# The two projections of 16 columns multiplied in split form, with high and low weights side by side in 32 columns

## The chip, the cores and the metric

The kernel runs on one core of one Trainium2 chip. The metric is the time of one execution on the device, in microseconds (us); lower is better. Engines are called as the profile calls them: PE is TensorE's matmul (PEld its weight load), DVE is VectorE, ACT is ScalarE, POOL is GpSimd, SP is SyncE, which here only issues DMAs.

## What is computed

Two transformer blocks on 256 rows of 1024 features. The first has, beside its wide projections, one of 16 columns, the low-rank factor of a gate; the second has, beside its wide ones, 16 columns of logits (8 `b_logit`, 8 `a_logit`) for the gated delta rule. Cut to what matters:

```
h = rms_norm(x, norm_w)
proj = h @ w_in                          # (256, 1024) @ (1024, 6160)
(gq, gk, gv, glr, hq, hf, hi, xq, gate) = split(proj)      # glr has 16 columns
glr_up = glr @ gla_w_gate_up + gla_b_gate                  # (256, 16) @ (16, 512)
gla_log_a = log_sigmoid(glr_up) / 16

h2 = rmsnorm(h, n[2])                    # 272 rows: 16 meta tokens and 256
proj = h2 @ w_in_2
u_f, u_sc, u_qkv, z, b_logit, a_logit, gate_logit = split(proj)   # 8 + 8 columns
beta = sigmoid(b_logit);  g = -exp(A_log) * softplus(a_logit + dt_bias)
```

## The kernel before

Activations lie transposed in SBUF: features on the 128 partitions in `KT` = 8 tiles, rows of the sequence along the free axis (256, or 272 with the meta tokens). Weights come in panels of 128 output columns by 1024 features (512 KB), through a ring of four slots: SP loads `raw`, ACT rounds it to float32r (`whi`, L722), POOL takes the rest (`wlo` = `raw` - `whi`, L622, two instructions of 128x512 for one panel). Activations are split in the same way into `xh` and `xl`. A wide output is then three float32r products for each of the eight tiles (`whi`x`xh`, `whi`x`xl`, `wlo`x`xh`), 24 matmuls summed in one PSUM bank `panel` (`products`, L1659). Four banks `panel` and four banks `aux` are used in rotation. Where a slot or a bank comes free, and where one is full, is told by semaphores (`lo_ready`, `passed`, `bank_free`, `aux_free`, `aux_full`).

The order of steps is written out by hand in `first_schedule` and `mixer_schedule`; each engine walks the same list and does its own part of each step. The two narrow projections stand apart from the panels:

- `("lowrank",)` is the first step of the first list. PE multiplies plain float32: 8 matmuls with `wglr` (16 columns) as weights and `tmp`, the normed input, moving (L1783). The profile records each float32 matmul as two. DVE copies the result to `glr` (L1185). The step `("decay",)`, after the first 16 outputs, multiplies `glr` by `upw` (L1793).
- `("ba",)` stands in the second list behind `("qkv", 0)`, a step that computes three outputs abreast. PE multiplies `wba` by `h` in float32 (L1953), with 272 rows moving; DVE had scaled `wba` by the gains much earlier (L1178). DVE multiplies the result by `xrstd` into `ba` (L1378). `("logits",)` transposes `ba` four times on PE (L1960), `DVE` and `ACT` turn the logits into `grate` (last at L1389, semaphore `g_ready`), and `("cumulate",)` sums `grate` on PE (L1967, L1968).

Ahead of the first list DVE has a series of small instructions on `small1` (L1169 to L1173), then folds a gain vector (L1176) and scales `wba` (L1178). In the list its part of the outputs 0 to 3 is two instructions each on `f` and `k` (L1192, L1193). POOL splits the first panels of this stage (panels 4 to 7, outputs 0 to 3), then clears `s` (a MEMSET, L648), and goes on with panel 8. PE's own part of the first list begins behind these waits:

```
            pe.wait_ge(more_in, 11 * 16)
            pe.wait_ge(split_low, 8)
            for step in FIRST:
```

## Time and profile before

| | us |
|---|---|
| median of 3 runs (lowest, highest) | 1028.63 (1028.36, 1029.28) |
| the profiled execution, its own time | 1030.11 |
| its span, from the first to the last instruction | 1028.3 |
| PE busy | 1004.7 |
| POOL busy | 765.5 |
| DVE busy | 534.0 |
| ACT busy | 486.5 |

The profile is of one execution. Its span is 1.8 us shorter than that execution's own time, and that time is 1.5 us above the median of the three runs. Times in the rows below are counted from the start of the span. The engines work beside each other, so their busy times don't add up; the chain of waits tells which of them set the end at each moment.

### The profile page before, as it was taken

Reading aid. Unit: us, or ns where it says so; the run is one execution under the profiler, and the core shown is the slowest. Engines: PE = TensorE matmul, PEld = TensorE weight load, DVE = VectorE, ACT = ScalarE, POOL = GpSimd, SP = SyncE. Lnnn points to the kernel's source line nnn. Section 1 sums busy time; section 2 is a strip of 40 time slices with the busy share of each in tenths; the row PEclk is TensorE's granted clock in tenths of the full one; section 3 lists DMA queues with packets and bytes.
Section 4 is the critical chain, followed back from the end, with each engine's and each line's share of the span. In section 5 each row is a group of like instructions: output and inputs, shape, how many; then the busy total and the mean of one; then the engine's idle time right before and its main releaser. Section 6 shows DMA issues by size and latency. Waiting matters only on the chain.

```text
span 1028.3 us, 21621 instructions
## 1 busy us (share of the span) xinstructions
PE 1004.7 (98%) x8212; PEld 984.2 (96%) x8212; DVE 534.0 (52%) x898; ACT 486.5 (47%) x748; POOL 765.5 (74%) x602
## 2 busy tenths in 40 slices
PE   9999999999999999999999899999999989999996
PEld 7999999999999999999899899999999989999996
DVE  5925984457544444504755463466656464444203
ACT  6543324456654444444566534433255554444441
POOL 2896666657999888996586845577539929999993
PEclk9999999999999999999999899999999999999998
DMA  9563334343565555555462213433226726665561
GB/s 319 163 203 127 123 105 143 119 128 107 181 198 183 175 171 174 165 174 181 126 186 91 72 54 114 142 125 122 85 65 199 215 95 195 195 196 184 173 185 58
DMA packets 48330, 154.62 MB, mean 150 GB/s; under 512 B 6060, under 2 KB 11188, under 8 KB 48264
## 3 DMA queue, kind: packets, MB, share of 16 engines
q1 hardware_dynamic: 46112, 151.31, 47.3%
q10 hardware_dynamic: 2152, 2.38, 0.7%
q8 instruction: 48, 0.79, 0.3%
q14 instruction: 18, 0.15, 0.0%
HBM read 151.57 MB, written 2.10 MB: 149 GB/s over the span
## 4 chain that ended last, share of the span: by engine, by line
PE 88%; DVE 4%; ACT 3%; POOL 2%; issue 1%; DMA 1%; SPq 0%; DVEq 0%; ACTq 0%
PE panel L1659 69%; PE panel L1709 3%; PE aux L1812 2%; POOL wlo L622 2%; PE panel L1759 1%; DMA memk<-in_mem_panels 1%; PE aux L2058 1%; PE aux L2069 1%; PE panel L1745 1%; PE aux L2032 1%; DVE tmp L1080 1%; PE aux L2098 1%; PE aux L2107 1%; PE aux L2021 1%; PE aux L1929 1%
## 5 line engine op out<-in xcount | busy, mean ns | idle before, releaser
L622 POOL TENSOR_TENSOR wlo<-raw,whi 128x512 fp32r<-128x512 f32 x554 | 736.4, 1358 | 239.7 <-ACT whi L722 221.3
L1659 PE MATMUL panel<-xh,whi 128*128 128x256 f32 (+1 forms) x1440 | 417.9, 290 | 4.7 <-DVE xl L1069 4.1
L1659 PE MATMUL panel<-xh,wlo 128*128 128x256 f32 (+1 forms) x1440 | 411.1, 285 | 0.0
L1659 PE MATMUL panel<-xl,whi 128*128 128x256 f32 (+1 forms) x1440 | 410.4, 285 | 0.0
L722 ACT ACTIVATE whi<-raw 128x1024 fp32r<-128x1024 f32 x280 | 293.9, 1053 | 217.7 <-PE panel L1659 184.3
L1659 PEld LDWEIGHTS panel<-xh,whi 128*128 128x128 f32 x1440 | 273.7, 190 | 7.3 <-issue 4.2
L1659 PEld LDWEIGHTS panel<-xh,wlo 128*128 128x128 f32 x1440 | 273.5, 190 | 0.0
L1659 PEld LDWEIGHTS panel<-xl,whi 128*128 128x128 f32 x1440 | 272.9, 190 | 0.2
L1659 PE MATMUL panel<-hh,wlo 128*128 128x272 f32 (+1 forms) x352 | 100.4, 285 | 0.0
L1659 PE MATMUL panel<-hh,whi 128*128 128x272 f32 (+1 forms) x352 | 100.1, 284 | 0.0
L1659 PE MATMUL panel<-hl,whi 128*128 128x272 f32 (+1 forms) x352 | 99.9, 284 | 0.0
L1339 DVE TENSOR_TENSOR hid<-hid,sil 128x272 f32<-128x272 f32 (+1 forms) x44 | 50.4, 1146 | 44.1 <-ACT sil L898 44.1
L1120 DVE TENSOR_SCALAR tmp<-panel,vec 128x256 f32<-128x256 f32 (+1 forms) x24 | 11.7, 489 | 107.8 <-ACT sq L779 107.8
L1659 PEld LDWEIGHTS panel<-hh,whi 128*128 128x128 f32 x352 | 66.3, 188 | 0.0
L1659 PEld LDWEIGHTS panel<-hl,whi 128*128 128x128 f32 x352 | 66.3, 188 | 0.0
L1659 PEld LDWEIGHTS panel<-hh,wlo 128*128 128x128 f32 x352 | 66.2, 188 | 0.0
L1335 DVE TENSOR_TENSOR hid<-panel,xrstd 128x272 f32<-128x272 f32 (+1 forms) x44 | 19.0, 432 | 55.9 <-PE panel L1659 55.9
L1341 DVE TENSOR_TENSOR hl<-hid,hh 128x272 f32 (+1 forms) x44 | 30.4, 691 | 32.9 <-ACT hh L900 32.9
L900 ACT ACTIVATE hh<-hid 128x272 f32 (+1 forms) x44 | 18.7, 425 | 57.7 <-DVE hid L1339 57.7
L1659 PE MATMUL panel<-mixh,whi 128*128 128x256 f32 x128 | 36.4, 284 | 0.0
L1659 PE MATMUL panel<-mixl,whi 128*128 128x256 f32 x128 | 35.8, 280 | 0.0
L1659 PE MATMUL panel<-mixh,wlo 128*128 128x256 f32 x128 | 35.8, 280 | 0.0
(328 smaller groups left out, 1580.4 us busy)
## 6 DMA issues: line engine op xcount, KB each, us to landing
raw<-in_panels SPq DMA_DIRECT2D x232, 512.0 KB, 3.6
raw<-in_down SPq DMA_DIRECT2D x32, 448.0 KB, 3.2
raw<-in_down SPq DMA_DIRECT2D x16, 512.0 KB, 3.4
memk<-in_mem_panels SPq DMA_DIRECT2D x4, 512.0 KB, 7.9
memx<-in_mem SPq DMA_DIRECT2D x4, 256.0 KB, 5.7
h<-in_x SPq DMA_DIRECT2D x1, 1024.0 KB, 8.7
spill<-h ACTq DMA_DIRECT2D x1, 1024.0 KB, 4.6
h<-spill ACTq DMA_DIRECT2D x1, 1024.0 KB, 7.2
```

The costliest lines, as they stand in the source:

```text
L622: ins = nc.gpsimd.tensor_tensor(wlo[:, slot, half], raw[:, slot, half], whi[:, slot, half].bitcast(f32), ALU.subtract)
L722: A(whi[:, slot, :], raw[:, slot, :], ACT.Copy).then_inc(hi_ready, 1)
L900: A(hh[:, bass.ds(tile, 1), 0:w].rearrange("p a s -> p (a s)"), hid[:, pair, 0:w], ACT.Copy).then_inc(hid_high, 1)
L1080: TT(tmp[:, t, 0:w], tmp[:, t, 0:w], bc(rstd[:, 0:w], 1, len(tiles[m])), ALU.mult).then_inc(weighed, 1)
L1120: TS(tmp[:, i, 0:w], pb[o % 4][:, 0:w], vcol("gains", at0 + i), factor, ALU.mult, ALU.mult)\
L1335: TT(hid[:, pair, 0:w], pb[2 * pair + 1][:, 0:w], xrstd[:, 0:w], ALU.mult)\
L1339: TT(hid[:, pair, 0:w], hid[:, pair, 0:w], sil[:, pair, 0:w], ALU.mult).then_inc(hid_ready, 1)
L1341: TT(hl[:, bass.ds(tile, 1), 0:w].rearrange("p a s -> p (a s)"), hid[:, pair, 0:w], hh[:, bass.ds(tile, 1), 0:w].rearrange("p a s -> p (a ...
L1659: ins = M(bank[:, 0:w], wt[:, slot, P * t:P * t + P], x[:, kk, c0:c0 + w], start=first and m == 0 and n == 0, stop=last and m == len(pairs ...
L1709: ins = M(pb[(o + rt) % 4][:, 0:2 * P], x[:, kk, P * rt:P * rt + P], wt[:, r:r + 2, P * kk:P * kk + P], start=kk == 0 and n == 0, stop=kk ...
L1745: ins = M(pb[o % 4][:, 0:ROWS], mem_panel(i)[:, P * kk:P * kk + P], memg[:, kk, :], start=kk == 0, stop=kk == KT - 1)
L1812: ins = M(bank[:, P * m:P * m + P], k[:, hd, blk], q[:, hd, blk], start=True, stop=True)
```

## The change

Both narrow projections are done with float32r products. DVE writes a new tile `slim` of 8 x 32 columns: the rounded weights in columns 0 to 15, the rest in columns 16 to 31 (`split_slim`: a rounding copy, a wait for it, a subtraction). PE multiplies `slim` by `xh` and by `xl`, 16 matmuls with 32 weight columns, into 32 partitions of the bank (`slim_products`). The high and the low half are added where the result is used next: `upw` is loaded twice, one copy under the other, so that the product with the 32 rows of `glr` is the sum; and the four transposes of `ba` become four float32 matmuls with a constant of 32 x 16 (`both_parts`, new columns of `sel`). `ba` is now made from `xh` and `xl`, which hold the gains already, so `wba` is not scaled. `slim` is one tile for both: it is filled from `wglr` ahead of the first list and from `wba` once the first product has been read.

The step `("lowrank",)` moves behind the outputs 0 and 1.

```
-    steps = [("lowrank",)]
-    steps += [("out", i) for i in range(16)]
+    steps = [("out", 0), ("out", 1), ("lowrank",)]
+    steps += [("out", i) for i in range(2, 16)]
...
-            TT(wba[:], wba[:], bc(vec[:, VEC_AT["gains"] + 16:VEC_AT["gains"] + 24], 2, 16), ALU.mult).then_inc(wba_scaled, 1)
+
+            def split_slim(n, w_):
+
+                CP(slim[:, :, 0:16], w_[:]).then_inc(slim_high, 1)
+                dve.wait_ge(slim_high, n)
+                TT(slim[:, :, 16:32], w_[:], slim[:, :, 0:16].bitcast(f32), ALU.subtract).then_inc(slim_low, 1)
+
+            split_slim(1, wglr)
...
-                    CP(glr[:], bank[0:16, 0:ROWS]).then_inc(aux_free[n % 4], 1)
+                    CP(glr[:], bank[0:32, 0:ROWS]).then_inc(aux_free[n % 4], 1)
+                    split_slim(2, wba)
...
-                    TT(ba[:], bank[0:16, 0:LEN], xrstd[0:16, :], ALU.mult).then_inc(aux_free[n % 4], 1)
+                    TT(ba[:], bank[0:32, 0:LEN], xrstd[0:32, :], ALU.mult).then_inc(aux_free[n % 4], 1)
...
+            def slim_products(bank, n, w):
+
+                pe.wait_ge(slim_low, n)
+                for kk in range(KT):
+                    for m, x in enumerate((xh, xl)):
+                        ins = M(bank[0:32, 0:w], slim[:, kk, :], x[:, kk, 0:w], start=kk + m == 0, stop=kk == KT - 1 and m == 1)
+                return ins
...
-                    for kk in range(KT):
-                        ins = M(bank[0:16, 0:ROWS], wglr[:, kk, :], tmp[:, kk, 0:ROWS], start=kk == 0, stop=kk == KT - 1)
-                    ins.then_inc(aux_full, 1)
+                    slim_products(bank, 1, ROWS).then_inc(aux_full, 1)
...
-                    pe.wait_ge(wba_scaled, 1)
-                    for kk in range(KT):
-                        ins = M(bank[0:16, 0:LEN], wba[:, kk, :], h[:, kk, :], start=kk == 0, stop=kk == KT - 1)
-                    ins.then_inc(aux_full, 1)
+                    slim_products(bank, 2, LEN).then_inc(aux_full, 1)
...
-                        ins = nc.tensor.transpose(bank[0:CH, 16 * c:16 * c + 16], ba[:, CH * c:CH * c + CH], ident[0:16, 0:16])
+                        ins = M(bank[0:CH, 16 * c:16 * c + 16], ba[:, CH * c:CH * c + CH], both_parts, start=True, stop=True)
```

DVE's list around the first narrow projection, before (`small_99` is `small1`, `aux` the bank of the narrow product):

```order
L1172 TENSOR_SCALAR small_99<-small_99 128x4 [waits dve_order]
L1173 TENSOR_SCALAR small_99<-small_99 128x4
L1176 TENSOR_TENSOR vec<-vec 128x8 [waits more_in,dve_order]
L1178 TENSOR_TENSOR wba<-wba,vec 128x128
L1185 COPY glr<-aux 16x256 [waits aux_full]
L1192 TENSOR_SCALAR f<-f,small_99 128x256 [waits bank_free0]
```

and now:

```order
L1179 TENSOR_TENSOR vec<-vec 128x8 [waits more_in,dve_order]
L1184 CAST slim<-wglr 128x8x16
L1186 TENSOR_TENSOR slim<-wglr,slim 128x8x16 [waits slim_high]
L1203 TENSOR_SCALAR f<-f,small_100 128x256 [waits bank_free0]
L1204 TENSOR_SCALAR k<-k,small_100 128x256
L1203 TENSOR_SCALAR f<-f,small_100 128x256 [waits bank_free1]
L1204 TENSOR_SCALAR k<-k,small_100 128x256
L1195 COPY glr<-aux 32x256 [waits aux_full]
L1184 CAST slim<-wba 128x8x16
L1186 TENSOR_TENSOR slim<-wba,slim 128x8x16 [waits slim_high]
L1203 TENSOR_SCALAR f<-f,small_100 128x256 [waits bank_free2]
```

The scaling of `wba` has gone; two instructions on `slim` stand behind the folded gain, the second with a wait, and two more behind the copy to `glr`, which now comes after the `f` and `k` of outputs 0 and 1.

PE's list where the first narrow projection begins, before (`whi,memgh` and the like belong to the memory projection in front of the list):

```order
L1759 MATMUL panel<-whi,memgl 128x256
L1759 MATMUL panel<-wlo,memgh 128x256
L1783 MATMUL aux<-tmp,wglr 16x256 [waits split_low,more_in]
L1783 MATMUL aux<-tmp,wglr 16x256 x7
L1659 MATMUL panel<-xh,whi 128x256 [waits bank_free0,lo_ready]
```

and now, where the 48 matmuls of outputs 0 and 1 end:

```order
L1670 MATMUL panel<-xh,whi 128x256
L1670 MATMUL panel<-xl,whi 128x256
L1670 MATMUL panel<-xh,wlo 128x256
L1679 MATMUL aux<-xh,slim 32x256 [waits slim_low]
L1679 MATMUL aux<-xl,slim 32x256
```

Fifteen more like the last two follow the first of them, in turn. The narrow product has moved behind two panels and waits for `slim_low`, a semaphore of DVE; the outputs in front of it wait for `lo_ready`, a semaphore of POOL.

## Rows read from the trace of the kernel before

**Rows 1.** The page: busy time of PE, and the shares of the chain by engine.
```profile
PE 1004.7 (98%) x8212; PEld 984.2 (96%) x8212; DVE 534.0 (52%) x898; ACT 486.5 (47%) x748; POOL 765.5 (74%) x602
PE 88%; DVE 4%; ACT 3%; POOL 2%; issue 1%; DMA 1%; SPq 0%; DVEq 0%; ACTq 0%
```
**Rows 2.** Chain of waits: start us, us, what; around both projections.
```profile
35.35 3.56 PE aux L1783 x16
38.91 45.63 PE panel L1659 x384
...
286.68 193.32 PE panel L1659 x1536
...
496.50 3.77 PE aux L1953 x16
500.27 3.21 PE panel L1659 x24
503.48 0.24 PE aux L1960 x4
503.72 6.24 PE panel L1659 x48
...
509.96 0.20 PE aux L1967 x4
```
**Rows 3.** Timeline of POOL, 34 to 45 us: start us, us, what.
```profile
34.71 1.28 POOL L622 TENSOR_TENSOR wlo<-raw,whi 128x512 fp32r<-128x512 f32 x1
...
37.17 1.27 POOL L622 TENSOR_TENSOR wlo<-raw,whi 128x512 fp32r<-128x512 f32 x1
...
42.12 1.43 POOL L622 TENSOR_TENSOR wlo<-raw,whi 128x512 fp32r<-128x512 f32 x1
43.48 1.81 POOL L648 MEMSET s<- 128x2048 f32 x1
```
**Rows 4.** Timeline of DVE, 38 to 55 us.
```profile
38.49 1.20 DVE L1171 TENSOR_TENSOR small<-small 128x4 f32<-128x4 f32 x1
39.72 1.21 DVE L1172 TENSOR_SCALAR small<-small 128x4 f32<-128x4 f32 x1
40.85 0.16 DVE L1173 TENSOR_SCALAR small<-small 128x4 f32<-128x4 f32 x1
41.04 1.14 DVE L1176 TENSOR_TENSOR vec<-vec 128x8 f32<-128x8 f32 x1
42.10 0.28 DVE L1178 TENSOR_TENSOR wba<-wba,vec 128x128 f32<-128x128 f32 x1
...
42.82 2.62 DVE L1192 TENSOR_SCALAR f<-f,small 128x256 f32<-128x256 f32 x1
45.37 1.38 DVE L1193 TENSOR_SCALAR k<-k,small 128x256 f32<-128x256 f32 x1
...
54.48 0.41 DVE L1199 COPY k<-panel 128x256 f32<-128x256 f32 x1
```
**Rows 5.** Stretches: us, busy PE, PEld, DVE, ACT, POOL, granted clock, DMA share, GB/s.
```profile
578.90:582.40 3.50, 1.47 (x14) 1.31 (x12) 1.04 (x3) 2.77 (x7) 3.50 (x6) 0.98 0.52 150
582.40:595.90 13.50, 13.50 (x59) 12.80 (x59) 2.69 (x13) 1.24 (x2) 5.25 (x9) 0.50 0.13 40
824.50:828.00 3.50, 1.30 (x9) 1.13 (x9) 3.50 (x9) 1.84 (x5) 0.00 (x0) 1.00 0.81 269
828.00:831.40 3.40, 3.20 (x16) 3.20 (x16) 3.40 (x8) 3.32 (x10) 0.00 (x0) 0.50 0.03 11
```
**Rows 6.** Timeline of DVE (and one row of POOL), 498 to 510 us.
```profile
499.14 0.50 DVE L1408 SCALAR_TENSOR_TENSOR qkv<-panel,vec,qkv 128x271 f32<-128x271 f32 x1
500.31 0.43 DVE L1378 TENSOR_TENSOR ba<-aux,xrstd 16x272 f32<-16x272 f32 x1 [0.66 <-PE aux L1953]
...
509.10 0.19 DVE L1389 SCALAR_TENSOR_TENSOR small<-small 68x32 f32<-68x32 f32 x1
...
498.60 10.02 POOL L622 TENSOR_TENSOR wlo<-raw,whi 128x512 fp32r<-128x512 f32 x8 [17.48 <-ACT whi L722]
```

More of the change, by code:

```diff
@@ L286, in build @@
         eye17 = at("eye17", take(SUB * SUB), [P, SUB, SUB])
-        sel = at("sel", take(57), [P, 57])
+        sel = at("sel", take(73), [P, 73])
         late = take(2048)
         masks = at("masks", late, [P, 8, P], i32)
-        upw = at("upw", late + 1024, [16, 512])
+        upw = at("upw", late + 1024, [32, 512])
+        slim = at("slim", late + 1664, [P, KT, 32], f32r)
         wglr = at("wglr", late + 1536, [P, KT, 16])
@@ L320, in build @@
         prob = at("prob", ar + 23552, [P, 2, 2, ROWS])
-        glr = at("glr", ar + 24576, [16, ROWS])
+        glr = at("glr", ar + 24576, [32, ROWS])
         small1 = at("small1", ar + 24832, [P, 64])
@@ L355, in build @@
         gt = at("gt", rstd_at, [P, 2, ROWS])
-        ba = at("ba", lnt_at, [16, LEN])
+        ba = at("ba", lnt_at, [32, LEN])
         yh = at("yh", tmp_at, [P, 4, ROWS], f32r)
@@ L383, in build @@
         row_in_block, block_of_row = sel[0:CH, 0:SUB], sel[0:CH, SUB:SUB + 4]
+        both_parts = sel[0:32, 57:73]
         matrix_of, block_of = sel[:, SUB + 4:SUB + 36], sel[:, SUB + 36:SUB + 40]
@@ L421, in build @@
         scaled = sem("scaled")
-        wba_scaled = sem("wba_scaled")
+        slim_high = sem("slim_high")
+        slim_low = sem("slim_low")
         down_squared = sem("down_squared")
@@ L2179, in constants @@
     m = np.arange(P)
-    sel = np.zeros((P, 57), f)
+    sel = np.zeros((P, 73), f)
     sel[:CH, :SUB] = np.arange(CH)[:, None] % SUB == np.arange(SUB)
@@ L2183, in constants @@
     sel[:, SUB + 4:SUB + 36] = m[:, None] % 32 == np.arange(32)
-    sel[:, SUB + 36:] = m[:, None] // 32 == np.arange(4)
+    sel[:, SUB + 36:57] = m[:, None] // 32 == np.arange(4)
+    sel[:, 57:] = m[:, None] % 16 == np.arange(16)
     eye = np.broadcast_to(np.eye(SUB, dtype=f), (P, SUB, SUB))
@@ L2253 @@
     arrays = {"panels": panels, "mem_panels": mem_panels[:4], "down": down, "x": rows(x["x"]), "mem": rows(x["mem"]), "meta": rows(x["meta_tokens_2"]),
-              "vec": np.concatenate([table[n] for n in VEC_AT], 1), "upw": x["gla_w_gate_up"],
+              "vec": np.concatenate([table[n] for n in VEC_AT], 1), "upw": np.concatenate([x["gla_w_gate_up"]] * 2),
               "wglr": glr.reshape(KT, P, 16).transpose(1, 0, 2), "wba": ba.reshape(KT, P, 16).transpose(1, 0, 2),
```

## The prediction

> **What bounds the kernel now.** I read the page first. PE is busy 98% of the span, and PE alone is 88% of the chain that ended last [rows 1]: a microsecond taken from PE's queue is a microsecond off the time, unless what PE does next is not ready. Then I read the chain of waits around the two projections [rows 2]. Both lie on it: sixteen recorded matmuls of 3.56 us at 35.35, sixteen of 3.77 us at 496.50, each between matmuls of panels without a gap. Third come the timelines of POOL and DVE beside the first [rows 3, 4], since the change puts DVE's work in front of PE's there; fourth the same for the second [rows 6]; last the stretches where TensorE's granted clock fell [rows 5], since the change can make PE idle.
>
> All sums below are against the profiled execution: span 1028.3 us, its own time 1030.11 us, which is 1.5 us above the median. They give a difference, which I add to the median, 1028.63 us. A measurement of this kernel can tell about 0.2%, 2.06 us, from no change.
>
> **The matmuls themselves.** A float32r matmul with 256 rows moving takes 45.63 / 384 = 0.119 us, one with 272 rows 193.32 / 1536 = 0.126 us [rows 2]. All of these have 128 weight columns; 32 columns are in no row. Bounds: 0.107 us for 256 rows, if only columns at 2.4 GHz counted (the clock granted there is full speed), and 0.2225 us (3.56 / 16, what each recorded half of a float32 matmul takes) if narrow float32r ran no faster than float32. I take 0.119 and 0.126, since number format and rows moving are those of the panels. Lowrank: 16 x 0.119 = 1.90 against 3.56 us. `ba`: 16 x 0.126 = 2.01 against 3.77. Saved on PE: 1.66 + 1.76 = 3.4 us at most. The logits give some back: four transposes took 0.24; four float32 matmuls are recorded as eight, and four records of such a kind (L1967) take 0.20 [rows 2], so 0.40, or 0.2 more.
>
> **The first place: lowrank moved.** Before, PE did lowrank from 35.35 to 38.91 with what was long ready, then outputs 0 and 1 to 38.91 + 48 x 0.119 = 44.6. Now it is different at three points.
>
> - Output 0 comes first and needs `wlo` of panel 4. POOL's second instruction for it is the one at 34.71, done at 35.99 [rows 3]. PE starts at about 36.1 instead of 35.35: idle 0.75. Output 1 needs panel 5, done at 37.17 + 1.27 = 38.4; PE asks at 38.95, so no wait. Outputs 0 and 1 end at 36.1 + 5.7 = 41.8.
> - Lowrank then needs `slim_low`. DVE's folding of the gain ends at 41.04 + 1.14 = 42.2, later than 41.8 already, and the two instructions on `slim` come behind it [rows 4]. Why DVE is late is in the rows: instructions on 4 elements take 1.2 us each. They end at 39.69, 40.93, 42.18, one POOL instruction (about 1.24 us) apart; each that begins after a wait is held to the next boundary between POOL's instructions, and one that follows without a wait goes straight through (L1173 0.16, L1178 0.28).
> - So the rounding copy, which follows without a wait, ends at about 42.3. The subtraction has a wait in front, so POOL's instruction of 42.12 to 43.55 gets in first. Bounds for the end of the subtraction: 42.65 (42.35 + 0.28 as L1178, if nothing holds it); 45.45 if it is held through POOL's MEMSET as well, as L1192 was, which began to wait at 42.82 and ended at 45.44, behind the MEMSET of 43.48 to 45.29 [rows 3, 4]. Between them is 43.7: the boundary at 43.5 and 0.2 us for its 128 elements. I take 43.7, because it is what L1171 and L1176, instructions of the same kind with two inputs in SBUF, did, while L1192 is a TENSOR_SCALAR.
>
> By that, PE idles from 41.8 to 43.8 and ends lowrank at 45.7 instead of having all this done at 44.6: **+1.1 us**. By the other bounds it is +0.05 and +2.85.
>
> The Trainium skill, page "SBUF — State Buffer", section "Who interferes with whom", says that a DVE instruction with two SBUF inputs contends with a GpSimd instruction that reads SBUF, not with one that only writes. No row here has such an instruction beside a MEMSET, so the trace doesn't show it; by the rule the sum is +1.1, and by the row of L1192 alone it would be +2.85.
>
> What is behind these waits: on PE the whole list, so the 1.1 us moves everything after it. On DVE, the `f` and `k` of outputs 0 and 1 start where they did (45.4), and the copy, the rounding and the subtraction behind them add at most 0.4 + 2 x 1.3 = 3.0 us. The first copy out of a bank (L1199) goes from 54.5 to about 57.5 [rows 4]; the output that needs this bank is output 8, at 45.7 + 6 x 2.85 = 62.8. Covered by 5 us; without that cover it would cost what it is late. Panels 6 and 7 are split before the MEMSET, by 43.55, ahead of need. The removed scaling of `wba` (0.28 us of DVE) and the doubled `upw` (32 KB more by DMA, first used behind output 15) cost and give nothing on PE's path; `glr` of 32 instead of 16 partitions changes no count of elements per partition or of columns moved.
>
> **The second place: ba.** `slim` was filled 440 us earlier: no wait. PE ends `ba` at 496.5 + 2.0 = 498.5 instead of 500.27, output `qkv 3` at 501.6, logits at 502.1, two outputs (6.24 us for 48) at 508.3. Their panels are split in time: POOL does eight instructions in 10.02 us from 498.60, so panels are ready at 501.1 and 503.6 [rows 6]. Then `cumulate` needs `g_ready`. DVE's chain towards it began with `ba` at 500.31, after 0.66 us of idle time; now it follows the last instruction of `qkv 0`, which ends at 499.64, so it begins 0.7 us earlier, and all of DVE and ACT behind it up to L1389 is in series: 509.29 becomes 508.6 [rows 6]. PE starts `cumulate` at about 508.8 (the 0.2 us is what the semaphore and a cold start of PE take) instead of 509.96: **-1.15 us**. PE's own work would have given 1.76 - 0.2 = 1.55. Ends: -0.7 (DVE's shift alone) and -1.6.
>
> **Sum:** +1.1 - 1.15 = -0.05 us: 1028.6. From the bounds without the clock: 0.05 - 1.6 = -1.55 to 2.85 - 0.7 = +2.15.
>
> **The clock** is not in this sum. Behind a stretch with 2.0 us of PE idle (3.50 - 1.47) the granted clock fell to 0.50 for 13.5 us; behind one with 2.2 us idle (3.50 - 1.30) for 3.4 us, in dense panels [rows 5]. That is 1.2 GHz instead of 2.4. The new idle time is 2.0 us, with 0.75 more six microseconds before. One stretch of 3.4 us at half clock in dense panels costs 1.7 us.
>
> **The rivals.**
> - *The clock falls at 43.8* after the wait of 2.0 us. For: both idle times of that size in the trace were followed by it. Against: in one the work before was light, and the new gap lies in full panels. -0.05 + 1.7: 1030.3. Chance 0.19.
> - *Slower: the subtraction waits for the MEMSET too.* Place: DVE's L1186 at 42.35. For: L1192 did exactly that. PE idles 3.7 us, more than either idle time before which the clock fell, so the 1.7 comes with it: 2.85 - 1.15 + 1.7 = +3.4: 1032.0. Each 0.1 us that `slim_low` comes behind 43.7 is 0.1 on the time, so with the clock at half it decides from about 44.1 on, without it only from 45.8. Chance 0.17.
> - *Nothing holds the subtraction*: +0.05 - 1.15 = -1.1: 1027.5. Against: L1171 and L1176. Chance 0.10.
> - *The change doesn't do what it says*: 32 weight columns run at the float32 pace. Lowrank is then another 1.66 later, `ba` saves nothing: 1.1 + 1.66 + 0.2 = +3.0: 1031.6. Against: every float32r row. Chance 0.05.
> - *The stretches at half clock from 582 and 828 us come out otherwise*, since everything there is moved by parts of a microsecond: one of 3.4 us more or fewer is 1.7 us, two are 3.4. 1025.2 to 1032.0; chance 0.12, of which 0.08 faster and 0.04 slower.
> - *All the saving that is left arrives*: with `slim_low` before 41.8, lowrank ends at 43.7 instead of 44.6, -0.9, and `ba` gives 1.55: -2.45, 1026.2. It needs a DVE that POOL doesn't hold, against L1171, L1172 and L1176 [rows 4]. Chance 0.04.
>
> **How the numbers follow.** My forecast, 1028.6, has 0.33. Within 0.2% (1026.6 to 1030.7) lie it, the clock alone and the unheld subtraction: 0.33 + 0.19 + 0.10 = 0.62. Slower: 0.17 + 0.05 + 0.04 = 0.26. Faster: 0.08 + 0.04 = 0.12. The range goes from 1026.4 (the forecast's lower bound, -1.55, and some scatter of runs) to 1032.2 (the MEMSET case and 0.2); it leaves out the last rival and the faster ends of the clock's case.
>
> **What would show it.** In the profile after: the 16 matmuls of L1679 take 1.9 and 2.0 us; PE idle about 0.7 before output 0; the subtraction L1186 ends near 43.7; a wait of PE for it of about 2.0 us; granted clock 1.00 in the 4 us after; PE waits about 0.4 us for `g_ready` at `cumulate`. I am wrong if the subtraction ends before 43 or behind 45, if the clock falls at 44, if narrow matmuls are slower than 0.13 us, or if the stretches at half clock later in the span have another length.

## The result, and the profile after

| | before | after |
|---|---|---|
| median of six runs each, one beside the other | 1028.95 us | 1034.78 us |
| lowest and highest of them | 1028.36, 1030.85 | 1032.98, 1036.30 |
| the profiled execution, its own time | 1030.11 us | 1032.98 us |
| its span | 1028.3 us | 1031.2 us |

The change makes the kernel slower: the ratio, of the means 1034.76 and 1029.32 us, is 1.0053, 95% interval 1.0039 to 1.0068. The prediction was 1028.6 us with a range up to 1032.2, so it missed on the slow side. The profiled execution is the quickest of the changed kernel (its six runs lie on two levels, near 1033 at a mean granted clock of 0.989 and near 1036 at 0.986), so the pair of profiles differs by 2.9 us where the medians differ by 5.8. In the experiments below, one execution of e2 took 2523.28 us and one of the kernel before beside it 1406.10 us; the ratios leave both out.

The page, in answer to [rows 1]: PE works 3.2 us less, near the 3.4 that the prediction had, though this is a net figure, since the half clock shown below lengthens some matmuls and spares others. PE's share of the chain is smaller; DVE's has grown from 4% to 6%.

```profile
PE 1001.5 (97%) x8216; PEld 984.7 (95%) x8216; DVE 539.2 (52%) x901; ACT 486.1 (47%) x748; POOL 765.6 (74%) x602
...
PE 86%; DVE 6%; ACT 3%; POOL 2%; issue 1%; DMA 1%; SPq 0%; DVEq 0%; ACTq 0%
```

The chain of waits around the first place, in answer to [rows 2] (start us, us, what):

```profile
40.42 1.34 DVE small L1176
...
42.97 1.81 DVE slim L1184
...
44.81 1.27 DVE slim L1186
...
46.12 3.26 PE aux L1679 x16
49.38 39.76 PE panel L1670 x336
89.14 1.07 PE aux L1810 x4
```

Where PE's matmuls ran without a gap before, the chain now goes through DVE: L1176 and its neighbours on a few elements, then the two on `slim`. PE gets `slim` at 46.1 us (forecast: 43.8), and its narrow product takes 3.26 us (forecast: 1.9). These are the timelines of DVE and of POOL there, in answer to [rows 4] and [rows 3]:

```profile
39.28 1.23 DVE L1175 TENSOR_SCALAR small<-small 128x4 f32<-128x4 f32 x1
40.42 1.33 DVE L1176 TENSOR_SCALAR small<-small 128x4 f32<-128x4 f32 x1
41.79 1.18 DVE L1179 TENSOR_TENSOR vec<-vec 128x8 f32<-128x8 f32 x1
42.90 1.88 DVE L1184 CAST slim<-wglr 128x128 fp32r<-128x128 f32 x1
44.81 1.26 DVE L1186 TENSOR_TENSOR slim<-wglr,slim 128x128 fp32r<-128x128 f32 x1
```

```profile
31.90 11.04 POOL L625 TENSOR_TENSOR wlo<-raw,whi 128x512 fp32r<-128x512 f32 x8 [3.34 <-ACT whi L725]
42.90 1.79 POOL L651 MEMSET s<- 128x2048 f32 x1
44.66 5.12 POOL L625 TENSOR_TENSOR wlo<-raw,whi 128x512 fp32r<-128x512 f32 x4
```

L1176 is the instruction that took 0.16 us before, as L1173. Here it took 1.33, from 40.42 to 41.75, beside the `wlo` instruction that POOL ran from 40.45 to 41.72 (a part of the merged row of eight); as the rows look, POOL got in first. L1179 ended at 42.97 instead of 42.18, although POOL itself ran 0.4 us earlier than before, so DVE had fallen back by one POOL instruction. That brought the rounding copy L1184 to the MEMSET: it is recorded from 42.90 to 44.78, the MEMSET from 42.90 to 44.69. The subtraction then met the next `wlo` instruction and took 1.26. The Trainium skill, page "SBUF — State Buffer", section "Who interferes with whom", says that DVE shares one pair of ports with GpSimd, as an exclusive lock, and that a copy or cast can take that pair by itself. The trace agrees: the copy took 1.88 us beside the MEMSET against 0.20 with POOL idle, in this same profile.

```profile
50.45 0.20 DVE L1184 CAST slim<-wba 128x128 fp32r<-128x128 f32 x1
```

PE was idle before output 0 and again before its first narrow matmul, and this is what the clock did (timeline of PE, then stretches: us, busy PE, PEld, DVE, ACT, POOL, granted clock, DMA share, GB/s):

```profile
35.74 0.36 PE L1670 MATMUL panel<-xh,whi 128*128 128x256 f32 x1 [1.20 <-POOL wlo L625]
...
46.12 0.42 PE L1679 MATMUL aux<-xh,slim 128*32 128x256 f32 x1 [4.46 <-DVE slim L1186]
```

```profile
41.66:46.12 4.46, 0.00 (x1) 0.00 (x1) 4.39 (x5) 1.82 (x3) 4.46 (x5) 0.92 0.75 236
46.12:49.50 3.38, 3.38 (x19) 2.83 (x20) 3.38 (x3) 0.00 (x0) 3.38 (x3) 0.60 0.29 73
49.50:53.00 3.50, 3.50 (x31) 3.50 (x31) 1.45 (x5) 0.70 (x3) 0.28 (x1) 1.00 0.67 232
```

PE was idle for 4.46 us behind the 48 matmuls of outputs 0 and 1, and the 16 narrow matmuls ran mostly at half clock. From the start of the last matmul of the memory projection to the step `decay` it is 89.14 - 34.26 = 54.88 us; before it was 84.54 - 35.07 = 49.47. So the first place cost **5.4 us**, against a forecast of 1.1. The last matmul of the memory projection, after and before, and the start of `decay` before:

```profile
34.26 0.28 PE L1778 MATMUL panel<-wlo,memgh 128*128 128x256 f32 x1
35.07 0.28 PE L1759 MATMUL panel<-wlo,memgh 128*128 128x256 f32 x1
84.54 1.07 PE aux L1793 x4
```

The second place, in answer to [rows 6] and [rows 2] (timeline of DVE, then the chain):

```profile
504.46 0.42 DVE L1389 TENSOR_TENSOR ba<-aux,xrstd 32x272 f32<-32x272 f32 x1
...
513.03 0.56 DVE L1399 SCALAR_TENSOR_TENSOR small<-small 68x32 f32<-68x32 f32 x1 [1.93 <-ACT small L945]
```

```profile
514.48 29.56 PE panel L1670 x240
...
554.05 1.06 PE aux L2014 x8
...
581.01 1.92 PE aux L2035 x8
```

The panels behind `cumulate` start at 514.48, 4.18 us later than before (510.30), and 4.90 us late was the stage on arrival (493.46 against 488.56): `ba` gave **0.7 us** (forecast 1.15). The attention's chunk steps, which the prediction did not speak of, start 4.17 us late (554.05 against 549.88) and end 4.91 late (581.01 against 576.10): **0.74 us** lost, just what `ba` had given. Behind them the stretch at half clock is shorter, in answer to [rows 5]:

```profile
587.90:598.20 10.30, 10.30 (x51) 10.30 (x50) 1.43 (x7) 0.00 (x0) 4.53 (x6) 0.51 0.16 52
```

10.3 us instead of 13.5: this returned 1.64 us, read at the same matmuls behind it (613.39 against 610.12, which is 3.27 late and no longer 4.91). The sum for the profiled pair: +5.4, the memory projection ended 0.8 earlier (this moves by up to 1 us from profile to profile), -0.7 for `ba`, +0.7 for the chunk steps, -1.6 for the clock, and -0.1 for the rest: +2.9 us of span. Without the memory projection's end and the clock behind 588 us, 5.4 us remain, 0.5% of the kernel. That this equals the measured ratio proves little: the length of that half clock differs between kernels for a reason that no run here isolates (13.7 us in e3, 10.2 in e2, e6, e7 and e12), and no execution near 1036 us was profiled.

### The profile page after: what moved, and what is told of

Read it like the earlier page. It is cut to its first block, busy times and chain, and to the rows that moved or that the text cites. A ratio compares the mean times of both kernels' runs of the same rounds, so it can differ in the third digit from the quotient of the medians.

```text
span 1031.2 us, 21632 instructions
## 1 busy us (share of the span) xinstructions
PE 1001.5 (97%) x8216; PEld 984.7 (95%) x8216; DVE 539.2 (52%) x901; ACT 486.1 (47%) x748; POOL 765.6 (74%) x602
## 4 chain that ended last, share of the span: by engine, by line
PE 86%; DVE 6%; ACT 3%; POOL 2%; issue 1%; DMA 1%; SPq 0%; DVEq 0%; ACTq 0%
PE panel L1670 68%; PE panel L1728 3%; PE aux L1829 2%; POOL wlo L625 2%; PE panel L1778 1%; DMA memk<-in_mem_panels 1%; PE aux L2072 1%; PE aux L2083 1%; PE panel L1764 1%; PE aux L2046 1%; PE aux L2112 1%; PE aux L2121 1%; DVE tmp L1083 1%; PE aux L1736 1%; PE aux L1946 1%
```

## The experiments

Theories at the start: (A) the loss is the wait for `slim_low` and the clock behind it; (B) the moved place alone, or the narrow matmuls, cost it; (C) something behind it does. Fifteen kernels ran (e1 to e15), each beside the kernel before on the same chip. `keep_clock(bank, n)` in some of them is `n` float32 products of ones into a bank that nobody reads; the profile records each as two. In this table "front" is the time from the start of the last matmul of the memory projection to `decay`, "chunks" the time of the chunk steps, both in the profile.

| kernel | ratio to before (95%) | median us (before) | front us | chunks us |
|---|---|---|---|---|
| before | | | 49.47 | 26.22 |
| after | 1.0053 (1.0039, 1.0068) | 1034.78 (1028.95) | 54.88 | 26.96 |
| e1 narrow product behind output 4 | 1.0001 (0.9992, 1.0010) | 1029.53 (1029.74) | 49.19 | 26.96 |
| e2 move alone, float32 | 1.0008 (0.9999, 1.0018) | 1030.16 (1029.74) | 50.55 | 26.39 |
| e3 products in PE's wait | 1.0046 (1.0030, 1.0061) | 1033.92 (1029.74) | 53.56 | 26.97 |
| e4 only `ba` split | 1.0000 (0.9991, 1.0009) | 1029.57 (1029.74) | 49.47 | 26.97 |
| e5 `slim` made earlier | 0.9995 (0.9986, 1.0004) | 1029.16 (1029.29) | 49.00 | 26.98 |
| e6 `slim` earliest, narrow product first | 0.9984 (0.9975, 0.9993) | 1027.55 (1029.29) | 47.87 | 26.96 |
| e7 MEMSET moved | 1.0057 (1.0040, 1.0075) | two runs, 1034.00 and 1036.36 (1029.29) | 54.64 | 26.97 |
| e8 products at gather, kernel before | 0.9961 (0.9949, 0.9974) | 1025.22 (1029.29) | 49.47 | 26.24 |
| e9 = e6 and e8 | 0.9944 (0.9931, 0.9956) | 1024.54 (1029.21) | 47.79 | 26.95 |
| e10 after, products at gather | 1.0019 (1.0005, 1.0033) | 1030.51 (1029.21) | 50.79 | 26.98 |
| e11 e4, `ba` delayed | 1.0011 (1.0002, 1.0020) | 1030.86 (1029.21) | 49.47 | 26.95 |
| e12 after again | 1.0068 (1.0054, 1.0082) | 1036.04 (1029.62) | 55.10 | 26.97 |
| e13 rounding copy alone earlier | 1.0014 (1.0005, 1.0023) | 1030.90 (1029.62) | 50.67 | 26.97 |
| e14 `sel` 73 wide | 0.9994 (0.9985, 1.0003) | 1028.53 (1029.62) | 49.46 | 26.22 |
| e15 two more on DVE | 1.0009 (1.0000, 1.0018) | 1030.12 (1029.62) | 49.47 | 26.96 |

### e1: take the wait away, keep everything else

```
-    steps = [("out", 0), ("out", 1), ("lowrank",)]
-    steps += [("out", i) for i in range(2, 16)]
+    steps = [("out", i) for i in range(5)] + [("lowrank",)]
+    steps += [("out", i) for i in range(5, 16)]
```

> The changed kernel with the step lowrank behind output 4 instead of output 1; nothing else differs. Theory W (the loss is PE waiting for the subtraction on slim, which DVE ends at about 46 us, and the half clock behind that wait): outputs 2 to 4 fill the wait, PE asks for slim at about 50, so no wait and no half clock there; against the changed kernel 4.7 + 1.3 = 6.0 us less, against the kernel before -0.2 to -1.5 us. Rival N (32 weight columns make the matmuls slow, or the logits do): about as the changed kernel, +4 to +7. Rival L (the loss lies in the later stretches at half clock, whose place and length change): no definite gain, granted clock mean stays below that of the kernel before.

Measured: no change against before (1.0001), so 5 us better than the change. The 0.2 to 1.5 us below the kernel before that were expected did not come: the front gives 0.28 (49.19 us), and the chunk steps take 0.74 (26.96). The chain has the 16 narrow matmuls without a wait and at full clock, 0.116 us each:

```profile
50.95 1.85 PE aux L1679 x16
```

So narrow split matmuls are no slower than those of panels, and the loss hangs on the place of the product in the list.

### e2: the move alone

```
-    steps = [("lowrank",)]
-    steps += [("out", i) for i in range(16)]
+    steps = [("out", 0), ("out", 1), ("lowrank",)]
+    steps += [("out", i) for i in range(2, 16)]
```

> The kernel before with only the step lowrank moved behind output 1: plain float32, no slim. Theory W: PE waits only for panel 4 ahead of output 0, 0.7 to 1.1 us, and lowrank takes its 3.56 us unhindered: +0.7 to +1.1 us against the kernel before. If the move itself (order of banks, of panels) were the loss: +4 or more.

Measured: 1.08 us more in front (1.0008). The move itself costs about a microsecond, because output 0 waits for panel 4 where the narrow product had filled that time; the forecast had 0.75. It is not what cost 5.4.

### e3: products in PE's wait

```
                     aux_open(n)
+                    keep_clock(ab[3], 18)
                     slim_products(bank, 1, ROWS).then_inc(aux_full, 1)
```

> The changed kernel with 18 matmuls of ones into a free bank, whose result nobody reads, ahead of the narrow product, so that PE is busy for about 4.3 us of the wait for slim. Theory W with the clock in it: the wait is as long (slim ends at about 46), the granted clock stays 1.00, lowrank takes 1.9 instead of 3.26 us: 1.4 us less than the changed kernel (+3 to +4 against the kernel before). If the clock had no part: the same time as the changed kernel within 0.3 us. If the later stretches at half clock are what spreads the runs of the changed kernel by 3 us, they spread these too.

Measured: the narrow product takes 2.05 us instead of 3.26, the front 1.3 us less (53.56), and the time is 1033.92 with no run near 1036 (four runs). The ratio, 1.0046, is not clear of the changed kernel's 1.0053, so the 1.3 us is a reading of two profiles. Of the 5.4 us, the clock is 1.3 by this. The other 4.1 are PE's two waits, 1.20 us for panel 4 and 4.46 for `slim_low`, less the 1.6 or so that split form saves on the matmuls.

### e4: only ba split

The kernel before with `("ba",)` and `("logits",)` as in the change, `slim` filled from `wba` ahead of the first list, and lowrank in float32, first.

> Only the second narrow projection in split form; lowrank stays first and plain float32. slim is filled from wba where wba was scaled. Theory W: no wait in front; ba gives what it gave in the changed kernel's profile, 0.7 us (4.90 us behind at 493, 4.18 at 514): -0.7 us, to -1.5 if DVE's chain to g_ready is not held by POOL. Rival N: 0 to +1.

Measured: nothing (1.0000), where 0.7 us less was expected. The profile shows that gain and its loss: the panels behind `cumulate` start 0.80 us earlier than before (509.50; 0.10 of it had come with the stage), the chunk steps too (549.08), and they end at 576.05 against 576.10.

### e5, e6: make slim earlier

e5 puts `split_slim(1, wglr)` with its wait for `more_in` behind DVE's copies of the memory projection, ahead of the small instructions. e6 puts it ahead of the last four of these copies, and the narrow product first in the list again:

```
+            dve.wait_ge(more_in, 11 * 16)
+            split_slim(1, wglr)
             for i in range(4, 8):
                 mem_out(i)
...
+    steps = [("lowrank",)]
+    steps += [("out", i) for i in range(16)]
```

> The changed kernel with the first split of slim (rounding copy and subtraction) moved on DVE from behind the folded gain to the end of the copies of mv, 1.6 us of idle time of DVE; lowrank stays behind output 1. Theory W: slim is ready at about 38, before PE asks at 41.5; lowrank ends at about 43.4 instead of 49.4, no half clock there: 5.5 to 6.5 us less than the changed kernel. What is left of the gain (0.5 us at the first place, 0.7 at ba) is then spent on the 0.8 us that the stage from 549 to 576 took longer in the kernels with a split ba: within 1 us of the kernel before. Rival: the second split of slim or the 32 columns cost something that these kernels all carry; then it stays above the kernel before by 1 us or more.

> As e5_front, but the split of slim one group earlier (ahead of the copies of mv) and lowrank first in the list again, so that its 1.9 us cover the wait for panel 4. Theory W: at the end of output 1 PE is 1.7 us ahead of the kernel before, behind ba 2.4; 0.8 are spent from 549 to 576: about -1.6 us against the kernel before (ratio 0.998 to 0.9995). If the stage from 549 to 576 takes up any lead of PE: 0.

Measured: e5 takes all of the loss away (0.9995) and e6 is quicker than the kernel before, 0.9984. In e6, DVE does both instructions nearly in time for PE, and PE has no wait for panel 4, since the narrow product fills it as it did before:

```profile
33.44 0.21 DVE L1171 CAST slim<-wglr 128x128 fp32r<-128x128 f32 x1
33.68 1.27 DVE L1173 TENSOR_TENSOR slim<-wglr,slim 128x128 fp32r<-128x128 f32 x1
```

```profile
35.09 2.02 PE aux L1679 x16
37.12 45.44 PE panel L1670 x384
82.56 1.07 PE aux L1810 x4
```

The front is 1.60 us shorter than before, where the count of matmuls gives 1.66. The subtraction ends at 34.95, and PE's first narrow matmul starts 0.40 us behind the start of the last one of the memory projection, where it was 0.21 before: this place has no room to spare.

### e7: the MEMSET moved

```
-            nc.gpsimd.memset(s[:], 0.0).then_inc(s_zero, 1)
...
                 if step[0] == "out":
                     ahead(IN_P + step[1])
+                if step == ("out", 3):
+                    nc.gpsimd.memset(s[:], 0.0).then_inc(s_zero, 1)
```

> The changed kernel with POOL's MEMSET of s behind the split for output 3 instead of behind panel 7. Theory (the rounding copy is held by whatever POOL instruction runs, here the MEMSET): it is then held by a wlo instruction of 1.25 us instead of the MEMSET of 1.8, so slim ends 0.5 us earlier, at about 45.5, and the time is 0.5 us less than the changed kernel's, still +4 to +5 over the kernel before. If the MEMSET alone held it: the copy takes 0.2 us, slim ends at 44.2 and PE is 1.9 us earlier.

Measured: 1.0057, no better, in only two runs. With the MEMSET gone, POOL's next `wlo` instruction stands in its place and holds the rounding copy as well (1.36 us, then 1.25 for the subtraction). Counted from the last matmul of the memory projection, `slim` is full 0.5 us earlier, as expected, but the front is only 0.24 us shorter. The MEMSET as such is not the cause; a `wlo` instruction there does the same.

### e8: the clock at gather, in the kernel before

```
                     aux_open(aux("gather")[1])
+                    keep_clock(aux("gather")[0], 9)
```

> The kernel before with 9 matmuls of ones (about 2.1 us) into the free bank of the step gather, ahead of PE's wait of 2.03 us at 580. If that idle time is what brings the half clock of 582 to 596: the granted clock stays at 1.00, the 13.5 us at half clock go, and PE, which is on the chain there, is up to 6.7 us ahead, as far as DVE's inversion beside it lets it; -2 to -6 us, and the runs' two levels (1028.3 and 1029.9) become one. If the light matmuls before and after bring it: no change, or +0.1 for dummies that end late.

Measured: 0.9961. PE's idle 2.03 us ahead of the step gather became 18 recorded matmuls, and the 13.5 us at half clock behind it [rows 5] were gone in the profile. That profile is of the quickest of six executions (1022.64 us; the others reach 1027.44, at mean granted clocks from 0.993 to 0.996), so the two levels of the kernel before did not become one, and how much half clock the others kept is not shown. The first row is of the chain, the second a stretch:

```profile
579.09 2.01 PE aux L1628 x18
```

```profile
582.00:596.00 14.00, 14.00 (x107) 12.98 (x107) 8.31 (x27) 2.30 (x3) 7.35 (x8) 1.00 0.22 76
```

### e9: both gains together

e6 with the line of e8.

> The kernel after the change, with the first split of slim moved in front of DVE's last four copies of the memory projection, lowrank first in the list again, and nine idle products (1.1 us of PE work each half, written to a free bank) in PE's wait at the step gather. Theory, that each of the two causes acts by itself: the first change was worth 1.6 us (1027.5 against 1029.3) and the second 4.1 us (1025.2), so 1023.6 us, a ratio of 0.9945, PE without half clock between 582 and 596. Rival, that the earlier arrival at gather (by 1.6 us) puts PE's wait elsewhere and the nine products miss it: then PE still falls to half clock behind it and the time is near 1027.5.

Measured: **0.9944 (0.9931 to 0.9956)**, the ratio that was expected and the lowest median of the study, 4.7 us below the kernel before; the interval overlaps that of e8 (0.9949 to 0.9974). But the profile doesn't show the clock as expected: the products fill the wait, and half clock still comes, later and shorter (mean 0.76 between 582 and 596, against 1.00 in e8 and 0.51 before). So the ratio came out as expected in part by luck, and that the two gains add up by themselves is not shown.

```profile
582.00:596.00 14.00, 14.00 (x86) 13.44 (x86) 6.89 (x22) 1.06 (x1) 6.15 (x7) 0.76 0.19 49
```

### e10: the same products in the changed kernel

The changed kernel with the line of e8.

> The changed kernel as it is, plus the same nine products in the wait at gather. If the changed kernel's half clock behind gather is one stretch of 3.4 us shorter than before's (10 against 13.5 us), which returned 1.64 us to it, then taking that half clock away is worth 1.7 us less here than it was in the kernel before (4.1): about 2.4, 1032.4 us, ratio 1.0030 against before. The cost of the change with both cleaned is then 1032.4 - 1025.2 = 7.2 us, more than the 5.4 us measured. Rival, that the clock behind gather has nothing to do with it: the full 4.1 arrive, 1030.7, ratio 1.0014, and the cost stays 5.4.

Measured: 1.0019, which by itself can't tell what the products did, since the front came out otherwise. Eight of its twelve runs lie between 1028.16 and 1031.25 (mean clock 0.991 to 0.996), four between 1033.46 and 1035.13 (0.988 to 0.990). In the profiled one (1029.84) the front is the one that the prediction described:

```profile
40.70 0.16 DVE L1176 TENSOR_SCALAR small<-small 128x4 f32<-128x4 f32 x1
40.89 1.14 DVE L1179 TENSOR_TENSOR vec<-vec 128x8 f32<-128x8 f32 x1
41.95 0.21 DVE L1184 CAST slim<-wglr 128x128 fp32r<-128x128 f32 x1
42.20 1.24 DVE L1186 TENSOR_TENSOR slim<-wglr,slim 128x128 fp32r<-128x128 f32 x1
```

```profile
43.49 2.07 PE aux L1679 x16
45.56 39.76 PE panel L1670 x336
```

L1176 goes through at once, the rounding copy too, `slim` is full at 43.4, the clock stays at full speed there, and the front costs 1.3 us more than before. Between this profile and that of the changed kernel, L1176, an instruction on four elements per partition, is where the two part: +1.3 or +5.4 us.

At gather the products did not keep the clock here; half clock came behind them all the same:

```profile
586.10:596.20 10.10, 10.10 (x43) 8.77 (x41) 4.05 (x15) 1.06 (x1) 4.33 (x5) 0.50 0.16 52
```

It is shorter than in e13 below, a kernel without these products that reaches the end of the chunk steps at the same time (577.10 against 577.24): 13.6 us there. At the same matmuls behind it e10 is 1.41 us ahead (609.71 against 611.12).

### e12: the changed kernel again

> The changed kernel once more, word for word. In the profile of the changed kernel with products at gather, DVE's L1176 took 0.16 us and not 1.33, the two instructions on slim 0.21 and 1.24 us, slim was full at 43.4 as the prediction had it, and the time was 1029.8; in the first profile of the changed kernel L1176 was held by POOL, then the rounding copy by the MEMSET, and slim was full at 46.1. Theory, that which engine gets the port first at L1176 is decided anew in each execution: the runs fall in two groups, near 1029 to 1030 and near 1033 to 1036, and with the six runs of before, all in the upper group, the lower one is the rarer. Rival, that it depends on the program's text and not on the execution: all runs lie between 1033 and 1036.5.

Measured: 1033.41 to 1037.02, all five in the upper group, and in the one profile L1176 at 1.33 us and the first `slim` full at 46.1 again. With the six runs of the result that is eleven of eleven by their times. So my theory, that each execution of this program throws the coin anew, isn't borne out for the changed kernel; why e10, which has the same text up to that place, took the short way in its profiled execution, stays open. Over the profiles of all kernels, that instruction took 0.16 us in five (before, e5, e10, e14, e15) and 1.33 in twelve.

### e13: which of the two instructions on slim is held

```
             for i in range(4, 8):
                 mem_out(i)
+            dve.wait_ge(more_in, 11 * 16)
+            CP(slim[:, :, 0:16], wglr[:]).then_inc(slim_high, 1)
             dve.wait_ge(lb_exp, 1)
...
-            split_slim(1, wglr)
...
+            slim_rest(1, wglr)
```

`slim_rest` is the wait for `slim_high` and the subtraction, the last two lines of `split_slim`.

> The changed kernel with the rounding copy of wglr alone moved up, behind DVE's copies of the memory projection (35.6 us, in its idle time); the subtraction stays where it was, ahead of the first list, now behind L1179 and with its semaphore long given. Where L1176 is held, L1179 ends at about 42.9 to 43.5 and the subtraction stands beside POOL's MEMSET (43.2 to 45.0 or so). Theory A, that the MEMSET holds this form too (two inputs in SBUF), as it held the TENSOR_SCALAR on f and the rounding copy: slim full at about 45.0, PE idle 3.4 us, 1.1 us less than in the changed kernel: 1033.5. Theory B, that a MEMSET, which only writes, does not hold an instruction with two inputs in SBUF: 0.3 us, slim full at about 43.2, PE idle 1.5 us or so, 2.8 us less and perhaps the clock's 1.7 too: 1030 to 1032.

Measured: 1.0014, theory B. DVE, then POOL:

```profile
40.60 1.33 DVE L1178 TENSOR_SCALAR small<-small 128x4 f32<-128x4 f32 x1
41.97 1.19 DVE L1181 TENSOR_TENSOR vec<-vec 128x8 f32<-128x8 f32 x1
43.08 0.28 DVE L1187 TENSOR_TENSOR slim<-wglr,slim 128x128 fp32r<-128x128 f32 x1
43.28 1.75 DVE L1209 TENSOR_SCALAR f<-f,small 128x256 f32<-128x256 f32 x1
```

```profile
43.06 1.82 POOL L651 MEMSET s<- 128x2048 f32 x1
```

L1178 was held here as L1176 was in the changed kernel, so DVE is late by the same step. But the subtraction, with both inputs in SBUF, went through in 0.28 us inside the MEMSET, and the TENSOR_SCALAR behind it, with one, was held to the MEMSET's end. The kernel before's scaling of `wba`, also with two inputs in SBUF, took the same 0.28 us inside the MEMSET in the profiles of e2 and e8. PE waits for `slim_low`:

```profile
43.41 0.30 PE L1685 MATMUL aux<-xh,slim 128*32 128x256 f32 x1 [1.58 <-DVE slim L1187]
```

That is 1.58 us instead of 4.46, so about 2.9 us of the wait lie at the rounding copy: held by the MEMSET, it then delivered the subtraction to the next `wlo` instruction. The front costs 1.2 us more than before (50.67): waits of 1.09 us for panel 4 and 1.58 for `slim_low`, less the saving on the matmuls. The sentence of the Trainium skill that the prediction weighed (page "SBUF — State Buffer", section "Who interferes with whom": two SBUF inputs contend only with a GpSimd instruction that reads) is borne out by this row. The prediction had looked at the wrong instruction of the pair.

### e11, e14, e15: why the chunk steps are longer

e11 is e4 with `keep_clock(bank, 8)` ahead of `ba`'s own products. e14 is the kernel before with `sel` 73 columns wide. e15 is the kernel before with

```
-            TT(wba[:], wba[:], bc(vec[:, VEC_AT["gains"] + 16:VEC_AT["gains"] + 24], 2, 16), ALU.mult).then_inc(wba_scaled, 1)
+            for a, b in ((0, 2), (2, 4), (4, 8)):
+                ins = TT(wba[:, a:b], wba[:, a:b], bc(vec[:, VEC_AT["gains"] + 16 + a:VEC_AT["gains"] + 16 + b], 2, 16), ALU.mult)
+            ins.then_inc(wba_scaled, 1)
```

> The kernel with only ba split, and eight idle products (1.8 us, as much as the split saves) ahead of ba's own. It arrives where the kernel before does: cumulate at 510.3, the chunk steps at 549.9. Theory, that the chunk steps take 0.74 us longer only because everything arrives 0.8 us earlier against POOL's panels: they take 26.2 us as before, end at 576.1, and DVE's first am comes 5.3 us behind their start. Rival, that it is the form of ba (its 32 partitions, the float32 products of the logits, slim in SBUF) that makes them longer: 26.95 us, end at 576.85, time 0.75 us above the kernel before. By the theory the time is that of the kernel before, 1029.3 to 1029.7.

> The kernel before with sel 73 columns wide and no other edit: every tile allotted behind it lies 64 bytes further on. The chunk steps took 26.2 us in all kernels without the split ba and 26.96 in all with it, whenever they arrived. Theory A, that the place of tiles in SBUF makes it: 26.96 here, first am 4.91 us behind the start of the stage, time 0.7 us above the kernel before. Theory B, that it is something else: 26.2 and 5.28, the time of the kernel before.

> The kernel before with DVE's scaling of wba written as three instructions on parts of it instead of one: two instructions more on DVE's list, nothing else. Theory C, that DVE's number of instructions ahead of the chunk steps makes the difference there (in the kernels before, DVE starts its first am 0.59 us after its last instruction though ACT had ended 0.46 us earlier; in those with split ba, 0.1 us after ACT): 26.96 us and first am at 4.91 here. Otherwise 26.2 and 5.28, and the time of the kernel before.

Measured. e11 arrives at 550.11, as before, and still takes 26.95 us, so its time of arrival is not the cause; the time, 1.0011, is above before's as the rival had it. e14 has DVE's first `am` at 5.28 us as before and the time of before, so it isn't the place of tiles. e15, where nothing but the number of DVE's instructions 500 us earlier has changed, takes 26.96 us, like every kernel with the split `ba`. The rows of e15 (`am` at 4.92 us behind the stage's start at 549.87):

```profile
554.79 0.78 DVE L1433 TENSOR_TENSOR am<-dmat,aux 68x272 f32<-68x272 f32 x2 [0.22 <-ACT dmat L981]
...
559.45 0.61 DVE L1426 TENSOR_SCALAR dmat<-dmat 68x272 f32<-68x272 f32 x1
560.10 1.27 DVE L1427 TENSOR_SCALAR dmat<-dmat 68x272 f32<-68x272 f32 x1
```

and of the kernel before:

```profile
555.16 0.78 DVE L1431 TENSOR_TENSOR am<-dmat,aux 68x272 f32<-68x272 f32 x2 [0.59 <-ACT dmat L981]
...
559.46 0.30 DVE L1424 TENSOR_SCALAR dmat<-dmat 68x272 f32<-68x272 f32 x1
559.79 0.74 DVE L1425 TENSOR_SCALAR dmat<-dmat 68x272 f32<-68x272 f32 x1
```

In the kernel before DVE starts `am` 0.37 us later behind ACT than e15 does (0.59 against 0.22). Without that pause POOL gets its products 0.4 us earlier, so it starts its next pair of `wlo` instructions at 559.87 instead of 560.34, and they then stand in front of DVE's two short TENSOR_SCALARs: 0.61 and 1.27 us instead of 0.30 and 0.74. What DVE waits for there, the trace doesn't show. The kernel before has a packet of an instruction queue near this place, at 556.80 us; e2, e8 and e14, with the shorter chunk steps, have it too, while e15 and the kernels with the split `ba` have theirs 26 to 29 us earlier, counted from the start of the stage (row of the DMA view, 556 to 558 us of the kernel before; queue, kind: packets, MB, share):

```profile
q14 instruction: 1, 0.01, 1.5%
```

So the pause and the packet come and go together, at a place that moves with the number of DVE's instructions. That the pause is DVE's list of instructions being loaded is a guess and is not shown: the packet starts 1.6 us after `am` has begun. The time: e15 measured 1.0009 (1.0000 to 1.0018), and 0.74 us would be 1.0007; the interval reaches no change at all, so the 0.74 us is a reading of profiles, the same within 0.03 us in all twelve with the split `ba` and in e15.

## Why the prediction was wrong

- **The matmuls: right.** The narrow split matmuls take 0.116 us (e1) and 0.124 us in `ba` in the profile after, where 0.119 and 0.126 were taken. The rival of a float32 pace is out.
- **Output 0's wait: right in kind, too small.** 0.75 us was taken and 1.20 measured; e2 measured 1.08 for the whole move. In e10 and e13 `slim` came as forecast, PE waited 1.6 us for it where 2.0 had been taken, and the front cost 1.3 and 1.2 where the sum said +1.1.
- **"One that follows without a wait goes straight through": this is the step that failed.** It rested on L1173 at 0.16 and L1178 at 0.28, in one profile. It held for that instruction in five of seventeen profiles; the other twelve had 1.33. The first rounding copy has no wait in front of it either, and of the eight profiles in which it stands behind the folded gain it went straight through in e10 alone (0.21 us; 1.88 in six, 1.36 in e7). So a wait in front is not what makes the difference. As the rows look, such an instruction comes at the end of one that was itself held by POOL, and POOL's next may get in first; what decides it stays open. From there each thing followed: DVE one POOL instruction late, the rounding copy at 42.90 and not 42.1, beside the MEMSET, `slim` full at 46.07 and not 43.7, and a wait of PE of 4.46 us and not 2.0.
- **The bounds put the MEMSET at the wrong instruction.** The rival on the slow side had the subtraction held by the MEMSET from 42.35 (+2.85, with the clock 1032.0). The subtraction is not held by it (e13), the copy is, and behind a held copy the subtraction is held a second time, by a `wlo` instruction. The true end, 46.07, lies 0.6 us outside the upper bound of 45.45. The rival had the sign and PE's long wait right, but its total was too small (3.4, against 5.4 by the ratio), and its mechanism holds only in part. It was given 0.17.
- **The clock: right as a rival, size 1.3 for 1.7.** It fell with the idle time of 4.46 us, at half speed for 3.4 us (e3 is the same kernel with that time filled), and did not fall with the 1.6 us of e10 and e13, where `slim` came as forecast.
- **ba: right in kind, 0.7 for 1.15.** DVE's shift alone, the lower end that the prediction named, is what arrived: DVE's L1399 met POOL (0.56 us). The 0.2 us that the sum allows there for the semaphore and a cold start of PE stands in no row; after, PE starts 0.14 us behind DVE's last instruction (513.81 to 513.95).
- **Not foreseen: the chunk steps, +0.74.** They took back all that `ba` gave (e4), and follow DVE's number of instructions (e15).
- **The range** ended 2.6 us below the result. It was built from ends of single terms; two holds in a row and the clock behind them were not in it. The further 3 us of the runs near 1036 lie at a lower mean clock (0.986 for 0.989); no profile caught such a run, so where is open. In e3 half clock in front was avoided, and none of its four runs were up there.

## What to carry to other kernels

An operand made on an engine that shares a port with a busy neighbour should be made ahead of the need, with the neighbour's instructions counted in: with the same two instructions at 42 us the front cost 5.4 us, with them at 33 us and the narrow product first again it gave 1.6 (e6). Read how often a short instruction passes its neighbour from many rows or runs, not from one: the same instruction took 0.16 or 1.33 us, and what comes behind it inherits the difference. And if PE must wait with light work ahead of it, try giving it something to multiply: nine idle products were worth 4 us in e8, more than the whole change could have, but in e9 and e10 half clock came in spite of them, so look at the clock again after each change.

## What was not expected of the hardware

- A TENSOR_TENSOR with two inputs in SBUF ran in 0.28 us inside POOL's MEMSET, a TENSOR_SCALAR right behind it was held 1.75 us (e13).
- Two more instructions on DVE at 42 us removed a pause of 0.37 us at 555 us, and the stage got no quicker for it but 0.74 us longer in the profile, since POOL then came earlier into DVE's way (e15).
- Half clock behind 2.0 us of PE idle lasted 13.5 us in the kernel before, and 10.3 in the changed one. With that wait filled it lasted about 10 us in e10, 7 in e9 and none in e8: filling the wait is not by itself enough to hold the clock.
